# Modulation products of a two-block fp32 network moved to VectorE, with the gate stage's tiles ahead of its GLA steps

## The reference, cut to what matters

```python
proj = jnp.einsum('bsd,de->bse', h, w_in[layer])          # first block, ten groups
...
for i in range(DEPTH_2):
    g_norm, ada_w, ada_b, mp = layers[i]
    shift, scale, gate = jnp.split(jax.nn.silu(c) @ ada_w + ada_b, 3, axis=-1)
    shift_c, scale_c, gate_c = jnp.split(jax.nn.silu(c_ctx) @ ada_w + ada_b, 3, axis=-1)
    h = modulate(x, g_norm, shift[:, None], scale[:, None])
    hc = modulate(ctx, g_norm, shift_c, scale_c)
```

## Time and profile before

| | us |
|---|---|
| median of 3 runs | 1588.09 |
| lowest, highest | 1581.19, 1589.34 |
| the profiled execution | 1580.69 |
| its span, first to last instruction | 1578.5 |
| TensorE busy in the span | 1512.4 (96%) |
| VectorE, ScalarE, GpSimd busy | 760.2, 651.2, 534.7 |

### The profile page before, as it was taken

How to read it: one execution, slowest core, us unless ns; L and a number is a source line. 1 busy time by engine, 2 the same in 40 slices (tenths; PEclk the granted TensorE clock), 3 DMA queues, 4 the chain that set the end, 5 groups by cost and what they waited for, 6 DMA issues and landing times.

```text
span 1578.5 us, 21777 instructions
## 1 busy us (share of the span) xinstructions
PE 1512.4 (96%) x8776; PEld 1233.6 (78%) x8776; DVE 760.2 (48%) x1430; ACT 651.2 (41%) x1061; POOL 534.7 (34%) x472
## 2 busy tenths in 40 slices
PE   6999999999898999999999999999998989999997
PEld 5788988888777888888778987766786866666676
DVE  2338268274388225542465314777325445444423
ACT  6334243332432342223540315777415325555652
POOL 3344233323134384436342232433431330111231
PEclk9999999999999999999999999999998999999999
DMA  5533324234112145443212110210111220000111
GB/s 188 174 107 107 107 80 134 81 105 136 28 54 80 54 167 180 140 154 107 94 54 80 54 62 1 75 25 18 39 48 50 67 54 11 10 21 28 31 51 54
DMA packets 129315, 122.72 MB, mean 78 GB/s; under 512 B 11348, under 2 KB 125152, under 8 KB 129216
## 3 DMA queue, kind: packets, MB, share of 16 engines
q1 hardware_dynamic: 128960, 121.26, 24.4%
q10 hardware_dynamic: 256, 0.07, 0.0%
HBM read 116.87 MB, written 2.10 MB: 75 GB/s over the span
## 4 chain that ended last, share of the span: by engine, by line
PE 82%; DVE 11%; ACT 3%; issue 1%; POOL 1%; DMA 0%; ACTq 0%; DVEq 0%
PE ps L2059 10%; PE ps L2061 9%; PE ps L2060 9%; PE ps L2526 4%; PE ps L2547 3%; PE ps L2374 3%; PE ps L2536 3%; PE ps L2272 3%; PE ps L2271 2%; PE ps L2273 2%; PE ps L2365 2%; PE ps L2106 2%; PE ps L2134 2%; PE ps L2527 2%; PE ps L2051 2%; PE ps L2052 2%
## 5 line engine op out<-in xcount | busy, mean ns | idle before, releaser
L1157 POOL TENSOR_TENSOR w_lo<-raw,w_hi 128x512 fp32r<-128x512 f32 x320 | 419.8, 1343 | 757.6 <-ACT w_hi L668 699.3
L2059 PE MATMUL ps<-h_hi,w_hi 128*128 128x512 f32 x632 | 252.9, 400 | 4.1 <-POOL w_lo L1157 2.5
L2060 PE MATMUL ps<-h_lo,w_hi 128*128 128x512 f32 x632 | 246.9, 391 | 0.0
L2061 PE MATMUL ps<-h_hi,w_lo 128*128 128x512 f32 x632 | 246.9, 391 | 0.0
L668 ACT ACTIVATE w_hi<-raw 128x2048 fp32r<-128x2048 f32 (+1 forms) x77 | 145.5, 1889 | 131.6 <-PE ps L2061 49.0
L2059 PEld LDWEIGHTS ps<-h_hi,w_hi 128*128 128x128 f32 x632 | 119.5, 189 | 33.0 <-issue 6.3
L2061 PEld LDWEIGHTS ps<-h_hi,w_lo 128*128 128x128 f32 x632 | 119.1, 188 | 25.5
L2060 PEld LDWEIGHTS ps<-h_lo,w_hi 128*128 128x128 f32 x632 | 119.6, 189 | 23.2
L1948 DVE CUSTOM_DVE_ANT_0 prob_b<-ps,no_mask 128x768 f32<-128x768 f32 x64 | 61.0, 954 | 72.7 <-PE ps L2527 72.7
L1099 ACT ACTIVATE pT_b<-ps 128x512 f32<-128x512 f32 x96 | 52.1, 594 | 71.3 <-PE ps L2536 71.2
L2051 PE MATMUL ps<-w_hi,h_hi 128*128 128x256 f32 x256 | 73.7, 288 | 0.0
(11 more groups left out here) (450 smaller groups left out, 3391.9 us busy)
## 6 DMA issues: line engine op xcount, KB each, us to landing
raw<-in_w_in_dram SPq DMA_DIRECT2D x32, 1024.0 KB
raw<-in_ada_w_dram SPq DMA_DIRECT2D x16, 1024.0 KB
raw<-in_a_w_in_dram SPq DMA_DIRECT2D x10, 1024.0 KB
raw<-in_w_in_dram SPq DMA_DIRECT2D x16, 512.0 KB
ada_w<-in_ada_w_dram SPq DMA_DIRECT2D x8, 1024.0 KB, 6.1
raw<-in_b_w_in_dram SPq DMA_DIRECT2D x5, 1024.0 KB
raw<-in_w_proj_a_dram SPq DMA_DIRECT2D x4, 1024.0 KB
raw<-in_w_proj_b_dram SPq DMA_DIRECT2D x4, 1024.0 KB
```

The lines of the kernel that those rows point to most:

```text
L1157: last = nc.gpsimd.tensor_tensor(w_lo[:, ph.w(s), p], raw[:, s % 2, p], w_hi[:, ph.w(s), p].bitcast(F32), ALU.subtract)
L2059: mm(ps[:, j, :], wh[:, k, c], xh[:, k, :], start=(k == 0), stop=False)
L2060: mm(ps[:, j, :], wh[:, k, c], xl[:, k, :], start=False, stop=False)
L2061: last = mm(ps[:, j, :], wl[:, k, c], xh[:, k, :], start=False, stop=(k == KT - 1))
```

## The change

1. `ada` strips leave the list `HEAD_STRIPS` and the `raw` buffers. All 24 strips are done by VectorE in halves (`ada_half(i)`, half i of 48), the first 28 halves (14 strips) in the head stage from two half-strip buffers of their own (`ada_half_w`), the last ten strips in the merge stage. The tables say behind which tile a half stands (`HEAD_ADA`, `MERGE_ADA`), behind which tile TensorE sums a strip and ScalarE copies it (`HEAD_SUM`, `MERGE_SUM`), and behind which weight load SP issues a half's load (`HEAD_LOAD`). The 32 column product, its copy out and the operand `pick2` are gone.
2. In the gate stage `project` comes ahead of the GLA step of the same tile, as it does in the head stage.
3. The fifteen small loads are issued by SP behind `x` and the first weight strip.

```diff
-HEAD_STRIPS = ("q", "v", "ff", "ada", "ada", "fb", "i", "ada", "ada", "ga")
+HEAD_STRIPS = ("q", "v", "ff", "fb", "i", "ga")
 GATE_STRIPS = ("u|gb", "u|gb")
 MERGE_STRIPS = ("ma", "mb", "pa", "pb")
...
-HEAD_ADA, HEAD_SUM = {(1, 1): 3, (2, 0): 4, (5, 0): 7, (6, 0): 8}, {(2, 0): 3, (2, 1): 4, (5, 1): 7, (6, 1): 8}
-MERGE_SUM = {(1, 1): 0, (1, 4): 1, (1, 6): 2, (2, 0): 3, (2, 4): 4, (2, 6): 5, (3, 0): 6, (3, 4): 7}
-MERGE_LOAD = {(1, 0): 0, (1, 1): 1, (1, 2): 2, (2, 0): 3, (2, 1): 4, (2, 2): 5, (3, 0): 6, (3, 1): 7}
-N_ADA = 8
...
+N_HEAD_ADA, N_ADA = 14, 24
+HEAD_ADA = {(0, 2): (0,), (0, 3): (1,), (0, 4): (2,), (0, 5): (3,), (0, 6): (4,), (0, 7): (5,), (0, 8): (6,), (0, 9): (7,),
+            (0, 10): (8, 9), (1, 7): (10, 11, 12, 13), (1, 9): (14,), (1, 10): (15,), (2, 7): (16, 17, 18, 19), (2, 9): (20,),
+            (2, 10): (21,), (3, 7): (22, 23, 24, 25), (3, 9): (26,), (3, 10): (27,)}
+HEAD_SUM = {(0, 5): 0, (0, 7): 1, (0, 9): 2, (0, 10): 3, (1, 0): 4, (1, 9): 5, (1, 10): 6, (1, 11): 7, (2, 9): 8, (2, 10): 9,
+            (2, 11): 10, (3, 9): 11, (3, 10): 12, (3, 11): 13}
+HEAD_LOAD = {2: (0, 1), 4: (2, 3), 5: (4, 5), 6: (6, 7), 7: (8, 9), 8: (10, 11), 12: (12,), 13: (13, 14, 15, 16),
+             14: (17,), 18: (18,), 19: (19, 20, 21, 22), 20: (23,), 24: (24,), 25: (25, 26, 27)}
+MERGE_ADA = {(0, 6): 28, (0, 7): 29, (1, 1): 30, (1, 2): 31, (1, 3): 32, (1, 4): 33, (1, 5): 34, (1, 6): 35, (2, 1): 36,
+             (2, 2): 37, (2, 3): 38, (2, 4): 39, (2, 5): 40, (2, 6): 41, (3, 0): 42, (3, 1): 43, (3, 2): 44, (3, 3): 45,
+             (3, 4): 46, (3, 5): 47}
+MERGE_SUM = {(1, 1): 14, (1, 4): 15, (1, 6): 16, (2, 0): 17, (2, 4): 18, (2, 6): 19, (3, 0): 20, (3, 3): 21, (3, 5): 22,
+             (3, 7): 23}
+MERGE_LOAD = {(1, 0): 14, (1, 1): 15, (1, 2): 16, (2, 0): 17, (2, 1): 18, (2, 2): 19, (3, 0): 20, (3, 1): 21, (3, 2): 22,
+              (3, 3): 23}
 OUT_STRIPS = ("o", "o")
...
-        ada_sb = [at(f"ada_sb{n}", [P, STRIP], F32, b) for n, b in enumerate((r_s + 10 * KB,))]
-        ada_w = at("ada_w", [P, 2, 2048], F32, r_y)
-        ada_acc = at("ada_acc", [P, 2, STRIP], F32, r_s + 16 * KB)
...
+        ada_half_w = [at(f"ada_half{n}", [P, KT // 2, STRIP], F32, b) for n, b in enumerate((r_s + 4 * KB, r_yb + 8 * KB))]
+        ada_strip_w = at("ada_strip", [P, 2, 2048], F32, r_y)
+        ada_acc = [at(f"ada_acc{n}", [P, 2, STRIP], F32, r_s + b * KB) for n, b in enumerate((10, 16))]
...
+            def ada_loads(k):
+                for i in HEAD_LOAD.get(k, ()):
+                    h = i % 2
+                    if i >= 2:
+                        sp.wait_ge(s_ada, 8 * (i - 1))
+                    sp.dma_start(ada_half_w[h][:, :, :], ada_cols(i // 2)[:, h * KT // 2:(h + 1) * KT // 2, :]).then_inc(s_aw[h], 16)
+
+            def heads_it(it, s0=0, s1=None):
+                for s, kind in list(enumerate(HEAD_STRIPS))[s0:s1]:
+                    src = w_in[:, :, it * STRIP + IN[kind]:(it + 1) * STRIP + IN[kind]]
                     load(heads, it, s, [(k_of(raw, s % 2), src)])
-
+                    ada_loads(heads.k(it, s))
...
-            for name, (a, n) in ROW.items():
-                row = t[name]
-                while len(row.shape) > 1:
-                    row = row.rearrange("a b c -> (a b c)" if len(row.shape) == 3 else "a b -> (a b)")
-                act.dma_start(vec_rows[a:a + n, :], row.rearrange("(k p) -> k p", p=P)).then_inc(s_const, 16)
-            for n, name in enumerate(("ln_w", "ln_b")):
-                act.dma_start(ln_rows[n * GCH:(n + 1) * GCH, :], t[name].rearrange("a b -> (a b)").rearrange("(k p) -> k p", p=P)).then_inc(s_const, 16)
...
+            def ada_out(n):
+                act.wait_ge(s_adasum, n + 1)
+                nc.scalar.activation(ada[:, 4 * n:4 * n + 4], ps[:, 7, STRIP:STRIP + 4], ACT.Copy).then_inc(s_adaev, 1)
...
+            def ada_half(i):
+
+                n, half = i // 2, i % 2
+                if n < N_HEAD_ADA:
+                    dve.wait_ge(s_aw[half], 16 * (n + 2))
+                    w, acc = ada_half_w[half], ada_acc[0]
+                else:
+                    dve.wait_ge(s_aw[n % 2], 16 * (N_HEAD_ADA + (n - N_HEAD_ADA) // 2 + 2))
+                    w, acc = k_of(ada_strip_w, n % 2)[:, half * KT // 2:(half + 1) * KT // 2, :], ada_acc[1]
+                if i == 0:
+                    dve.wait_ge(s_setup, 2)
+                for x in range(KT // 2):
+                    k = half * KT // 2 + x
+                    if k == KT - 1 and n:
+                        dve.wait_ge(s_adasum, n)
+                    for o in range(2):
+                        part, c = ps[:, 6, o * STRIP:(o + 1) * STRIP], cT[:, 2 * k + o:2 * k + o + 1]
+                        if n or k:
+                            dve.wait_ge(s_ada, 16 * n + 2 * k + o - 1)
+                        if k == 0:
+                            v.tensor_scalar(part, w[:, x, :], c, None, ALU.mult).then_inc(s_ada, 1)
+                        else:
+                            v.scalar_tensor_tensor(part if k < KT - 1 else acc[:, o, :], w[:, x, :], c, part,
+                                                   ALU.mult, ALU.add).then_inc(s_ada, 1)
...
-            def ada_strip(ph, it, s, bank):
-                a = ph.a(it, s)
-                pe.wait_ge(s_raw[s % 2], 16 * ph.n(it, s) + 32 - 16 * (s % 2))
-                free = a - 1 if ph is heads else a
-                if free > 0:
-                    pe.wait_ge(s_adaev, free)
-                w = k_of(raw, s % 2)
-                for k in range(KT):
-                    q = k % 4 * 32
-                    last = mm(ps[q:q + 32, bank, 0:STRIP], cT[:, 2 * k:2 * k + 32], w[:, k, :], start=(k < 4), stop=(k >= 4))
-                last.then_inc(s_ada, 1)
-
-            def ada_sum(ph, it, s, bank):
-                pe.wait_ge(s_adasb, ph.a(it, s) + 1)
+            def ada_sum(n):
+                pe.wait_ge(s_ada, 16 * (n + 1))
+                if n:
+                    pe.wait_ge(s_adaev, n)
+                if n == N_HEAD_ADA:
+                    pe.wait_ge(s_yb, GCH)
                 for m in range(2):
-                    last = mm(ps[:, bank, STRIP + 2 * m:STRIP + 2 * m + 2], ada_mid(ph, it, s)[:, m * P:(m + 1) * P], pick2[:, :],
-                              start=True, stop=True)
+                    for o in range(2):
+                        c = STRIP + 2 * m + o
+                        last = mm(ps[:, 7, c:c + 1], ada_acc[n >= N_HEAD_ADA][:, o, m * P:(m + 1) * P], ones[:, 0:1], start=True, stop=True)
                 last.then_inc(s_adasum, 1)
...
+                        if (it, tt) in HEAD_SUM:
+                            ada_sum(HEAD_SUM[it, tt])
                         if not first:
                             if tt == 0:
                                 gla(it - 1, 0)
                             gla(it - 1, tt + 1)
-                        if (s, j) in HEAD_SUM:
-                            ada_sum(heads, it, HEAD_SUM[s, j], 6 + heads.j(HEAD_SUM[s, j]) % 2)
-                        if (s, j) in HEAD_ADA:
-                            if first and s == 1:
-                                weight_sums()
-                                pe.wait_ge(s_setup, 3)
-                            ada_strip(heads, it, HEAD_ADA[s, j], 6 + heads.j(HEAD_ADA[s, j]) % 2)
+                        if first and tt == 3:
+                            weight_sums()
...
                     tt = 2 * g + j
+                    project(gates, it, s, j, False)
                     if tt == 0:
                         gla(PAIRS - 1, 0)
                     if GATE_SLOT[tt] is not None:
                         gla(PAIRS - 1, GATE_SLOT[tt] + 1)
-                    project(gates, it, s, j, False)
```

145 lines of the change are left out of this document (42 added, 103 removed).

## The result

The changed kernel takes 1603.82 us (median of four runs, 1600.98 to 1605.01) and the kernel before 1588.07 (1581.19 to 1589.34). The ratio is 1.0121, with a 95% interval of 1.0096 to 1.0147: slower by 1.2%, where I had forecast no change, a time of 1588 and a range from 1573 to 1600. The profiled executions took 1605.01 us (span 1603.2) and 1580.69 (span 1578.5). Their spans lie 24.7 us apart, more than the medians (15.8), because the profiled one of before was a short one of its kernel (whose executions beside the experiments take from 1579.4 to 1590.2 us).

The account below looks back on a forecast made before the run. What counts is TensorE and what it waits for (last in the chain for 82%). Terms -1.1 - 1.2 - 23.0 + 11.2 + 6.6 - 2.0 + 0.8 + 9.4 = +0.7 us on 1588.1, about 1588; range 1573 to 1600.

Parts of the forecast that it names:

- Products off TensorE: Head stage: sixteen strips' old sum and product going give -23.0 us, fourteen new sums +11.2; net -11.8, from -4 to -15.
- Rival D: Slower: TensorE's clock falls at new waits behind tile 11 and the merge stage; up to +16 us, 1604; chance 0.23.
- (b): Theory formed after the profile, not in the prediction: each uncovered wait of TensorE brings a slow clock; no size given.
- The boundary behind tile 11: Head stage: TensorE's sum waits 2.2 us for VectorE's half in each of three iterations: +6.6 us, bounds 0 and 12.
- Halves on VectorE: Head stage: a half takes 3.2 us on VectorE and fits beside its other work, except behind tile 11.
- raw buffers: Head stage: with own buffers for modulation strips the one `w_lo` wait goes, -1.2 us; at most +13 from late halves.
- Gate stage: New order covers the 2.7 us `y_a` wait, but other waits come; stage 2 us shorter (-2), bounds -18.9 and +5.
- End of the merge stage: Behind the last merge tile the last sum's copy delays the first out tile: +9.4 us, bounds 0 and 12; extra sum +0.8.
- Start: Kernel start: ScalarE, freed of small loads, scales `x_tok` earlier, so transposes start earlier: -1.1 us, bounds -2 and +2.

## Why the prediction was wrong, step by step

**Products off TensorE: the step that failed.** I wrote that "a microsecond taken off TensorE in the head stage is a microsecond won". That holds in iteration 0, where VectorE has no GLA (-3.5 us measured, -3.0 forecast). In iterations 1 to 3 it doesn't. Between steps 3 and 8 of iteration 1 the old kernel took 41.5 us and the changed one 39.9: three products and two sums went, 3.8 us, and 1.5 were won; the rest became the waits for `vs` and `tot_a`. Over the three iterations the term was 12 x 1.44 = 17.3 us, and 8.0 of it came back as waits for VectorE (2.2 `vs`, 4.8 `tot_a`, 1.0 `v_tok`), with the slow clock on top. Rows 3 had shown the sign of it, small waits for `tot_a` (three, 0.7 us together): a wait of nearly nothing means that the cover just suffices, not that there is room. And the trace of before has one pair of `q_two` doublings at 3.48 us beside others at 1.28; I did not ask why. The bounds that I gave the term, -4 to -15, were also added up wrongly: by its own unit prices they are -2.7 to -14.4.

**The clock.** Rival D foresaw a slow clock behind new waits and gave 1597 to 1604, chance 0.23; 1603.8 came. But the waits it named are only part: in the head stage, step 0 to step 12, waits exceed the forecast by 5.8 us (2.2 `vs`, 4.8 `tot_a`, 1.0 `v_tok`, less 2.2 because only two of the three at tile 11 were long), and some 7.5 us are left for the clock, which agrees with 0.02 of 393 us. The granted clock is 0.50 in five places of this stage (201 to 204, 252 to 255, 310 to 313, 362 to 364 and 413 to 415), with twelve waits in it, so (b) does not hold for each wait. I had priced one such loss at 1.7 us, and with the wait of 2.0 us removed 3.9 came back, so 1.9 for the clock. D was right in kind and nearly in this price, and wrong about where most waits are: it has no wait for `vs` or `tot_a`, and takes its other 7 us from the gate stage, which is 3.8 above its term. That its 1604 is the time measured is luck.

**The boundary behind tile 11.** Forecast 2.2 us three times; measured 1.99 twice and 0.38 in iteration 3. Right, and the third place is no exception. VectorE ends its half at the same distance behind tile 11's start each time; what differs is TensorE. In iterations 1 and 2 tile 11 takes 5.4 us (first to last matmul) at full clock, the wait is 1.99 us and the clock falls behind it (0.50 from 201 to 204). In iteration 3 the clock falls inside tile 11 (0.50 from 413 to 415), which takes 7.0 us, and 0.38 is left to wait. From the tile's start to step 12 it is 8.6 to 8.9 us all three times. In the seven experiments that keep this sum behind tile 11 the wait is 1.98 or 1.99 behind a tile of 5.4 us and 0.38 to 0.43 behind one of 6.9 to 7.0, in whichever iteration; once, behind a tile of 8.1, there is none. So a single wait of this kind, between two profiles, says nothing of an edit.

**Halves on VectorE.** 3.2 us a half beside the GLA, as forecast; they delayed nothing but that sum. The **raw buffers** gave their 1.2 us.

**Gate stage.** Forecast -2, measured +1.8, and +1.3 by the order alone. (In the seven experiments that keep the new order the unchanged stage takes 148.3 to 152.1 us, so a single profile is good to some us here.) Idle time is nearly what I had added up (15.5 us in the window against 2.7 + 2 + 4 + 3 + 1 + 2 = 14.7), but in part by luck: the 2 us for the read-out of tile 0 and the 4 us ahead of the first `mix` did not come, and one wait of 4.2 for `w_lo` ahead of tile 2 stands in their place. The waits for `w_lo` that I had named come ahead of tiles 6, 8 and 12 as forecast, with 3.7, 1.9 and 2.7 us for my 3, 1 and 2. In all `w_lo` has 12.5 us where I had 6. With as much idle time as before (14.5 us) the stage could only get shorter through a faster clock. It got slower, 0.93 over the window against 0.97, which is worth 0.04 x 147 = 5.9 us; the sum has nothing for that, only the bound of +5. Behind tile 1 a wait of 2.5 and one of 4.2 us follow each other, and the clock there is 0.54 (439 to 448).

**End of the merge stage.** Forecast +9.4, measured +8.8, and undone by moving one copy. This was the best read part, since every engine's list there is short and fixed. The merge stage itself is 3.3 longer. In the kernels with the old gate order it is 1.7 longer, which is its two more sums (forecast 1.6); the other 1.6 come with the new gate order, whose late `w_lo` makes the first merge tile wait 1.0 us. The clock is 1.00 there before and after.

**Start.** Forecast -1.1, measured +0.7, or +0.6 over all profiled kernels. ScalarE scaled `x_tok` by 13.5 as forecast, and took up the strip at 13.44, so it had landed by then, also as forecast. The last small load landed at 14.9 and not 13.5: I had let the fifteen follow the strip with almost no time of their own.

**What stays open.** The 3.7 us in unchanged code at the end. From the end of the transposes to the end of the kernel the eight profiled kernels with the `xT` stall take 837.7 to 842.6 us, and the eight without it 833.9 to 835.7; about 3 us of that are the out tiles held by `h_lo`. Behind the second out tile TensorE's idle time is the same in both profiles (23.9 and 23.4 us), so the remainder is clock (0.99 before, 0.98 after). Whether the stall has to do with it is open: there the eight kernels without it take 823.1 to 824.8 us and six of those with it 826.8 to 828.7, but the other two, in which GpSimd's pieces were placed by a semaphore, 824.7 and 823.5. Why a stall should cost clock later was not tested.

## What to carry to other kernels

Before work is taken off the busiest engine, look at what it waits for right behind that work: if a chain on another engine lands just then, the work was cover, and removing it wins only the slack. A wait should be priced with the slow clock that may follow it: here a wait of 2.0 us cost 3.9. And the duration of one instruction that is two or three times that of its sisters may point to another engine's work beside it; moving such work by about 3 us in three iterations gave 12 us back.

## What the runs showed of the hardware

VectorE's elementwise work with two SBUF operands is held up by GpSimd's elementwise work one instruction at a time: 0.68 becomes 1.78 us, a pair 1.28 becomes 3.49, each instruction 1.1 us longer, about the length of one GpSimd piece (5.0 / 4 = 1.25 us), and GpSimd's four pieces go from 5.0 to 6.5. The Trainium skill, page "SBUF — State Buffer", section "Who interferes with whom", says that VectorE and GpSimd share a port pair under an exclusive lock, and that a VectorE instruction with two SBUF inputs contends with a GpSimd instruction that reads SBUF. The traces agree; that the lengths fit a lock better than a shared bandwidth is argued from them, not tested. The stretch also reaches a `TENSOR_SCALAR` with one SBUF tensor (`kf_new`, 0.47 to 1.50 us). I had not used that page for the prediction.

TensorE's granted clock: in the head stage it was 1.00 before the change, with waits of 0.2 to 1.2 us, and 0.98 after it, with waits of 0.4 to 2.0 us. In the slow stretches it is 0.50 (201 to 204, behind a wait of 1.99 us). Where such a slow stretch falls while TensorE would have had to wait anyway, as in tile 11 of iteration 3, it costs nothing: 8.6 us from the tile's start to step 12, against 8.7 and 8.9 with full clock in the tile.
